# RWKV block 0's front beside the projections, its inverses inside attention, attention's norm behind scan round 0

## The reference

```python
h = rms_norm(x) * (1 + sc1) + sh1
z = h @ w_in[l]
q_lat, kv_lat, k_pe = _split(z_mla, MLA_SIZES)
z_rwkv = centred_token_shift(z_rwkv, rwkv_mu[l])
r, k, v, xw_f, xw_b, xa_f, xa_b, xg = _split(z_rwkv, RWKV_SIZES)
y_mla = mla_group(...)     # per head softmax(q k) v, then rms_norm(o, out_norm)
y_rwkv = rwkv7_group(...)  # both directions:
#   w = exp(-exp(-softplus(-(w0 + tanh(xw) @ w2)) - 0.5)); a = sigmoid(a0 + xa @ a2)
#   k_d = k * (1 + (a - 1) * k_a); kk = k * k_k / |k * k_k|
#   state = state * w + (state @ -kk) (kk * a)^T + v k_d^T;  y = state @ r
x = x + gt1 * (jnp.concatenate([y_mla, y_rwkv], axis=-1) @ w_out[l])
h = rms_norm(x) * (1 + sc2) + sh2
x = x + gt2 * conv_ffn(h, ffn_w_up[l], ffn_conv_w[l], ffn_conv_b[l], ffn_w_down[l])
```

## Time and profile before

| | us |
|---|---|
| median of three runs | 1809.8 |
| lowest, highest | 1809.66, 1811.24 |
| the profiled execution | 1816.97 |
| its span | 1815.0 |
| TensorE busy in the span | 1625.1 (90%) |
| VectorE | 1013.9 (56%) |
| ScalarE | 737.1 (41%) |
| GpSimd | 289.7 (16%) |
| its mean granted TensorE clock | 0.948 |

### The profile page before, as it was taken

One profiled execution on the slowest core, in us unless ns is written; L12 is line 12 of the kernel. 1 busy time (PEld: TensorE's weight loads), 2 busy tenths in 40 slices (PEclk: granted clock), 3 DMA queues, 4 the chain that ended last, 5 costly groups with the idle time before them and its releaser, 6 DMA issues.

```text
span 1815.0 us, 29245 instructions
## 1 busy us (share of the span) xinstructions
PE 1625.1 (90%) x11880; PEld 1189.7 (66%) x11880; DVE 1013.9 (56%) x1533; ACT 737.1 (41%) x1203; POOL 289.7 (16%) x124
## 2 busy tenths in 40 slices
PE   2899877888989999989989988598889899999997
PEld 0776434656768888877757744266667688887885
DVE  6664669886336767754334243778841544445233
ACT  3443254665543322222234343457653333323222
POOL 1333000000122222212304310000003122222121
PEclk8899987999999999999989999699999999999999
DMA  7354210000225555533303310000003222222221
GB/s 302 115 183 163 84 47 1 3 2 2 77 87 185 186 185 185 185 128 131 137 23 119 93 55 1 1 3 3 3 2 116 70 93 92 92 92 92 93 92 70
DMA packets 34659, 163.08 MB, mean 90 GB/s; under 512 B 3841, under 2 KB 4097, under 8 KB 25857
## 3 DMA queue, kind: packets, MB, share of 16 engines
q1 hardware_dynamic: 34560, 161.65, 25.5%
HBM read 159.54 MB, written 2.10 MB: 89 GB/s over the span
## 4 chain that ended last, share of the span: by engine, by line
PE 55%; issue 28%; DVE 8%; ACT 4%; POOL 4%; DMA 0%; POOLq 0%; DVEq 0%; ACTq 0%
PE bank L505 8%; PE bank L507 7%; PE bank L506 7%; PE bank_pair L505 3%; PE bank_pair L507 3%; PE bank_pair L506 3%; POOL work_parts L1932 2%; PE bank L552 2%; PE bank L852 2%; PE bank L853 2%; POOL proj_weights_parts L1927 2%; PE bank_pair L609 1%; PE bank L830 1%; PE bank L666 1%; PE bank L868 1%
## 5 line engine op out<-in xcount | busy, mean ns | idle before, releaser
L505 PE MATMUL bank<-work_parts,y_mix_parts 128*128 128x512 f32 x792 | 316.1, 399 | 20.6 <-DVE work_parts L1698 10.3
L507 PE MATMUL bank<-work_parts 128*128 128x512 f32 x792 | 315.5, 398 | 0.0
L1711 DVE TENSOR_TENSOR work_parts<-work,y_mix_parts 128x1024 fp32r<-128x1024 f32 x66 | 169.6, 2569 | 257.8 <-ACT y_mix_parts L982 257.8
L1927 POOL TENSOR_TENSOR proj_weights_parts<-proj_weights,proj_weights_hi_parts 128x1024 fp32r<-128x1024 f32 x54 | 130.4, 2422 | 884.5 <-ACT proj_weights_hi_parts L978 796.0
L1932 POOL TENSOR_TENSOR work_parts<-work,y_mix_parts 128x1024 fp32r<-128x1024 f32 x66 | 159.1, 2410 | 608.5 <-ACT y_mix_parts L982 608.5
L982 ACT ACTIVATE y_mix_parts<-work 128x1024 fp32r<-128x1024 f32 x132 | 133.0, 1054 | 263.3 <-DMA work<-mlp_dram 253.6
L506 PE MATMUL bank<-work_parts,y_mix_parts 128*128 128x512 f32 x528 | 209.0, 396 | 0.0
L505 PEld LDWEIGHTS bank<-work_parts,y_mix_parts 128*128 128x128 f32 x792 | 150.6, 190 | 58.3 <-issue 24.0
L507 PEld LDWEIGHTS bank<-work_parts 128*128 128x128 f32 x792 | 150.4, 190 | 35.9
L505 PE MATMUL bank<-work_parts,proj_weights_hi_parts 128*128 128x512 f32 x272 | 112.5, 413 | 26.6 <-DVE work_parts L1698 24.4
L506 PEld LDWEIGHTS bank<-work_parts,y_mix_parts 128*128 128x128 f32 x528 | 100.5, 190 | 24.4
(11 more groups left out here) (279 smaller groups left out, 2991.0 us busy)
## 6 DMA issues: line engine op xcount, KB each, us to landing
work<-mlp_dram SPq DMA_DIRECT2D x66, 1024.0 KB, 4.9
work<-ada_dram SPq DMA_DIRECT2D x64, 512.0 KB, 4.7
proj_weights<-tiles_dram SPq DMA_DIRECT2D x57, 512.0 KB, 3.6
x_res<-ada_dram SPq DMA_DIRECT2D x24, 512.0 KB, 4.6
x_res<-x_dram SPq DMA_DIRECT2D x2, 2048.0 KB, 10.7
mixer_inputs<-ada_dram SPq DMA_DIRECT2D x8, 512.0 KB, 17.6
work<-mlaw_dram SPq DMA_DIRECT2D x4, 640.0 KB, 5.2
out_dram<-x_res SPq DMA_DIRECT2D x8, 256.0 KB, 2.2
```

The source lines that it names most:

```text
L505: mm(out, w_hi, x_hi, start=start, stop=False)
L507: return mm(out, w_lo, x_hi, start=False, stop=stop)
L1711: TTT(MW_L[q][:, 1], MW_IN[q][:, 1], plain(MW_H[q][:, 1]), ALU.subtract).then_inc(msp_v.sem, msp_v.one("l1"))
L1927: pool.tensor_tensor(ring_l[s], ring[s], plain(ring_h[s]), ALU.subtract).then_inc(spl_q.sem, spl_q.one(f"t{s}"))
```

## The change

Four things, the same in both layers:

- **Front of block 0 beside the projections.** `rwkv_early` of block 0 runs on TensorE ahead of tiles k of b = 1 and r of b = 2, in banks 7 and 0 (`EARLY_BANK`). ScalarE's and VectorE's steps of the front follow between the tiles of b = 1 to 3. The key norm of block 0 is taken at once; logarithms and exponentials of blocks 1 to 3 come behind the last tile. The low-rank weights are loaded at tile 5.
- **Inverses of block 0 and front of block 1 inside attention.** Pair 0: both triangles, the bonus product and the inverse from `inverse_in` to `inverse_32_mid`, in pieces at the end of VectorE's steps 3 to 9. Pair 1: the rest of the inverse in steps 0, 3 and 8, the running sums of block 1 in 1 and 2, its `rwkv_early` and exponentials, and `level_turn` ahead of the last product. K and V are copied out of PSUM by ScalarE instead of VectorE. The probabilities lie in the tile buffers `RING`, so three tiles of the output projection are loaded behind attention instead of ahead, and two of them are split in the last scan round. Both products with v use bank 4, the second behind the copy of the first.
- **No round -1.** Scan round 0 starts behind `level_rest`.
- **Norm of attention behind round 0.** Its squares are taken in round 0 (chunks 2, 3, 5, 6), sums and logarithm at the round's end in place of `keep_clock`, the exponential in round 1, the scalings in round 3 and `y_head` / `y_rest` behind them.

```diff
@@ TensorE, projections
+                        if b == 1 and i == 1:
+                            pe.wait_ge(lora_in, (l + 1) * 16)
+                            pe.wait_ge(in_a.sem, in_a.at("txw", l))
+                            pe.wait_ge(sta_a.sem, sta_a.at("ln2", l))
+                            rwkv_early(first, 0, 0)
+                        if b == 2 and i == 0:
+                            rwkv_early(first, 0, 1)
@@ TensorE, attention
+                    pe.wait_ge(att_a.sem, att_a.at("v1", it))
+                    if hp == 0:
+                        rwkv_triangle(first, 0)
+                    else:
+                        rwkv_early(first + 1, 1, 0)
                     pe.wait_ge(att_v.sem, att_v.at("rp3", it))
...
+                        if hp == 0 and i == 1:
+                            rwkv_triangle(first, 1)
+                        if hp == 0 and i == 4:
+                            rwkv_bonus(first)
+                        if hp == 1 and i == 3:
+                            rwkv_early(first + 1, 1, 1)
+                        if hp == 1 and i == 9:
+                            pe.wait_ge(att_a.sem, att_a.at("pt6", it))
+                            level_turn(first)
                         if i in (6, 9):
                             e = i // 9
                             pe.wait_ge(att_a.sem, att_a.at(f"pt{4 * e + 3}", it))
+                            if e:
+                                pe.wait_ge(att_v.sem, att_v.at("o0", it))
...
-                for cur in range(-1, RB):
+                pe.wait_ge(att_v.sem, att_v.at("o1", l * 2 + 1))
+                scan_gram(first, 0)
+                scan_tokens(first, 0, 0)
+                level_rest(first, 0, True)
+                for cur in range(RB):
                     rwkv_round(l, cur, cur + 1)
@@ TensorE, end of a round
+                    pe.wait_ge(sc_a.sem, sc_a.at(f"SA{NCH - 1}", it))
+                    if cur == 0:
+                        out_norm_sums(l)
...
+                    if cur == 0:
+                        pe.wait_ge(on_a.sem, on_a.at("ln", l))
+                    else:
+                        keep_clock(new, "join", 3)
+                    level_turn(new)
+                    level_rest(new, nxt, early)
@@ VectorE, attention
+                        if l == 0 and hp == 1 and i in (4, 6):
+                            ada_rest(8 + i // 2)
+                        if hp == 0 and i < 3:
+                            kk_norm(1 + i)
                         if 1 <= i < 9:
...
+                        if hp == 0:
+                            if i == 3:
+                                inverse_in(first)
+                                inverse_half(first)
+                            if i == 4:
+                                inverse_8(first, 1, 5)
+                            if i == 5:
+                                inverse_8(first, 5, 8)
+                                inverse_16_first(first)
+                            if i == 6:
+                                bonus_end(first, 0)
+                                inverse_16_second(first)
+                            if i == 7:
+                                inverse_16_end(first)
+                            if i == 8:
+                                inverse_32_first(first)
+                            if i == 9:
+                                inverse_32_mid(first)
+                        else:
+                            if i == 0:
+                                inverse_32_second(first)
+                            if i in (1, 2):
+                                decay_sum(first + 1, i - 1)
+                            if i == 3:
+                                inverse_32_end(first)
+                            if i == 8:
+                                for p in range(2):
+                                    for e in range(2):
+                                        dve.memset(XT[p][64 * e + 32:64 * e + 64, :, :, 0:32], 0.0).then_inc(lane_v, 1)
+                                inverse_out(first)
@@ ScalarE, rounds
+                    if cur == 0 and s in (2, 3, 5, 6):
+                        out_norm_square(l, (2, 3, 5, 6).index(s))
+                    if cur == 1 and s == 6:
+                        out_norm_scale(l)
...
+                    if not build and s in (0, 2):
+                        split_tile(l, NPROJ + s // 2)
+                    if not build and s in (1, 3, 5):
+                        if s == 1:
+                            act.wait_ge(on_v.sem, on_v.at("y3", l))
```

More of the change, by code:

```diff
@@ L567, in rwkv_level, with level_rest @@
                     own(lev_p, last, f"X{d}")
+            def level_rest(it, b, early):
                 scan_gram(it, 1)
@@ L589, in rwkv_level, with out_norm_sums @@
                 scan_tokens(it, b, 1)
+            def out_norm_sums(l):
+                for i in range(4):
+                    pe.wait_ge(on_a.sem, on_a.at(f"sq{i}", l))
+                    mm(PS[1][:, :], ones, ON_SQ[i], start=(i == 0), stop=(i == 3)).then_inc(on_p.sem, on_p.one(f"s{i}"))
             pairs = [(d, e) for d in D2 for e in range(2)]
@@ L742, in rwkv_round @@
                         tail_gate(old, cur - 1)
-                if scan:
-                    own(sc_p, last, "Y")
+                own(sc_p, last, "Y")
                 if build:
@@ L1833, in _ @@
+                    if l == 0 and hp == 0:
+                        ada_rest(8)
+                        ada_rest(9)
+                scan_ring(first, 0)
+                edge(l, 0, True)
+                for cur in range(RB):
+                    rwkv_round(l, cur, cur + 1)
                 dve.wait_ge(mod_kept, 20 if l == 0 else l * 24 + 24)
```

370 lines of the change are left out of this document (203 added, 167 removed).

## The result

The changed kernel takes 1760.8 us (median of 4 runs, 1758.3 to 1763.8) and the kernel before, on the same chip, 1810.5 us (1809.7 to 1812.1): ratio 0.9725, 95% interval 0.9705 to 0.9745. It is faster by 49.8 us; 1754.3 was predicted, with 1733 to 1780 as the range. The profiled executions differ by 58.0 us (spans 1815.0 and 1757.0).

A forecast was written before the change was run, and what follows sets the result against it. Projections and nearly attention were TensorE-bound; behind attention a serial chain left it waiting. Savings of 47.5 and 50.4 us less added costs gave -23.2 and -32.3, together -55.5 us from 1809.8: 1754.3 us, range 1733 to 1780.

The forecast's parts named there:

- What was removed: Stretch from attention's last copy to scan round 0: only about 9.2 us remain, removing 47.5 us in layer 0, 50.4 in layer 1.
- The margin of the front's last VectorE part: Behind the last projection: this 6.7 us part costs nothing, with margin under 1 us, in layer 1 3 us.
- Pair 0: First head pair of attention: VectorE's pieces delay the last scaling +6.1 and +3.9 us, half clock 1.7: +7.8 and +5.6.
- Pair 1: Second head pair of attention: VectorE's pieces, the wait before `level_turn` and slow clock stretch it by +12.3 and +8.3 us.
- the new wait: End of the second head pair: TensorE waits about 5 us for the inverse's transpose before `level_turn`, last product queued behind.
- The scan rounds: Scan rounds of each layer: the moved norm and weight splits add 2.5 us a layer, between 0 and 6.
- The term for round 3: Scan round 3: two weight-tile splits replace two head copies beside step 1's table load, where ScalarE arrives last: +1.2 us.
- The term for the join: Join of scan rounds 0 and 1: norm squares, four full products replacing clock keepers, and a table load: net +1.0 us.
- (D): ScalarE's table switches on or near the path: six cost 1.4 us more than shown, +8 us, 1762; chance 0.08.
- (E): Inverse inside attention: pieces show in full, 22.4 us instead of 6 to 10 a layer, +24 us, 1778; chance 0.05.
- (C): Attention: TensorE's clock falls to 1.2 GHz in a third of the four pairs, +31 us, 1785; chance 0.12.
- (A): Attention: stretched by VectorE's pieces as laid out in the main estimate, 1754 us; chance 0.52.

The follow-up runs named there:

- second profile: The changed kernel, unedited, run and profiled again beside the kernel before: ratio 0.9732 (0.9702 to 0.9762), 1763.0 us, span 1755.3.

## Why the prediction was right, and where it was not

**The direction and the mechanism** held step by step. What was removed came out within 0.6 us in both layers (-46.9 and -50.5 against -47.5 and -50.4): only the gram, the tokens and `level_rest` stand between the copy and round 0. The margin of the front's last VectorE part held too: the path from the last projection to the first score is as long as before, 14.3 us in both kernels, so all that comes ahead of attention comes in the projections, +2.3 and +2.5 us for the 1.7 charged.

**Pair 0** (+7.8 and +5.6 predicted; +7.1 and +3.8, second profile +6.4 and +2.1) is right as a sum and wrong in its two terms. The last scaling ends 28.7 and 26.7 us after the first score in both profiles, against 24.6 before: VectorE's share is +4.1 and +2.1, and I had charged +6.1 and +3.9. With the clock kept and nothing else changed, the whole pair is 4.1 us (34.5 - 30.4) and 2.4 us longer than before, which agrees. The 2.0 us too many do not lie in the pieces. From the third score on the trace shows no idle time of VectorE up to the last scaling, and its own work, the pieces and the conditioning take 25.5 us between the first maximum and the last scaling, where I had laid out 25.7. They lie at the start: I took the 2.9 us from the first score to the first maximum and 2 us of waiting from the kernel before, whose first scores ran at a lowered clock. The changed kernel has 2.0 and 1.1. The scores and the first maximum before, then the maximum after:

```profile
180.82 1.14 PE L852 MATMUL bank<-work 128*128 128x512 f32 x2 [2.11 <-DVE work L1797]
181.78 1.88 PE L853 MATMUL bank<-work 128*128 128x512 f32 x2
183.45 1.90 PE L852 MATMUL bank<-work 128*128 128x512 f32 x2
```
```profile
183.70 0.69 DVE L1801 TENSOR_REDUCE neg_max<-bank 128x1 f32<-128x512 f32 x1 [2.94 <-PE bank L853]
```
```profile
185.15 0.69 DVE L1932 TENSOR_REDUCE neg_max<-bank 128x1 f32<-128x512 f32 x1 [2.08 <-PE bank L887]
```

The clock's share at the pair's end is 37.5 - 34.5 = 3.0 us in layer 0 and 1.4 in layer 1 (second profile: 2.2 and none), where I had 1.7 for each. The two errors have opposite signs, so that the sum came out is in part luck.

**Pair 1** (+12.3 and +8.3; +12.9 and +7.4): the new wait is what the experiments show most clearly: a wait of 4.01 us ahead of `level_turn`, then 1.86 and 6.16 us of slowed work (5.86 in layer 1) for the 1.9 and 6.7 charged. Taking the wait away brings 5.9 and 3.7 us. The last scaling ends 27.6 us after the first score in layer 0 (second profile) and 25.6 in layer 1, where I had 27.6 and 25.1. In the first profile it ends after 29.2 in layer 0, since the clock also fell in the middle of the pair: the two rows of one score, 1.02 us each elsewhere, took 1.91 and 1.36. The two conditioning pieces, charged with 2.5 us, cost 2.1: 27.6 against 25.6 with them out, and 34.0 against 31.9 us for the pair with the clock kept.

**The scan rounds** (2.5 us a layer; 1.0 and 2.7, second profile 0.3 and 5.7). The term for round 3 (1.2 us) is seen in the traces: the two head copies that the splits push aside now stand behind the table load and ahead of the copy that the scan waits for, and TensorE waits 1.71 us where it had waited 0.68. Layer 1, before and then the second profile after:

```profile
1342.38 0.38 PE L666 MATMUL bank<-rstd,work 64*64 64x64 f32 x5 [0.68 <-ACT rstd L1115]
```
```profile
1280.23 1.15 ACT L1185 ACTIVATE work_parts<-y_mix 128x512 fp32r<-128x512 f32 x2
1281.27 0.28 ACT L1160 ACTIVATE rstd<-bank 128x128 f32<-128x128 f32 x1
1281.60 0.38 PE L674 MATMUL bank<-rstd,work 64*64 64x64 f32 x5 [1.71 <-ACT rstd L1160]
```

The kernel without the norm keeps this order and has the same 1.71 us. The term for the join (1.0 us) is not seen: with the norm left out the time is the same, and the first part of the rounds moves by 2.5 us between two profiles of the changed kernel (37.4 and 34.9 in layer 0). The rounds got longer by 3.7 and 6.0 us over both layers, so the rest of it, beyond two times 1.0 us, is the clock's or not explained. In round 3 of layer 1 the second profile stands at a granted clock of 0.72 and 0.83 in places where the kernel without the norm has 0.86 and 1.00, and a part of the rounds takes 42.3 us at 1.00 and 44.0 at 0.96 in one kernel or another. The rounds also go against what attention gains: over both layers they take 354.8 us before, 358.5 and 360.8 in the changed kernel, 360.3 and 359.5 in the two experiments that leave the order in pair 1 as it is (no norm; the multiplications alone), and 361.3 to 367.0 in all the others. No run shows why.

**The rivals.** (D) is out: a table load in the changed kernel ends where the next instruction begins, as in the earlier trace rows:

```profile
170.21 1.28 ACT L1323 ACT_TABLE_LOAD   x1
171.50 0.69 ACT L1323 ACTIVATE work<-bank,constants 128x512 f32<-128x512 f32 x1
```

The further drain of 1.38 us that the Trainium skill, "ScalarE: Activation LUTs", section "What ACT_TABLE_LOAD costs", states is not seen here: 170.21 + 1.28 = 171.49, and the activation ahead of the load ends at its start as well. So it is for 39 of the 41 loads of this trace, with 0.01 or 0.02 us behind them; the other two have 1.59 and 1.07 us. (E) is out as a case of its own: with the inverse in the open the kernel is 21.9 us slower. (C) came true in the clock and not in its price. I had written that a clock below 0.9 in attention would speak for it, and it stood at 0.86 and 0.84. Those figures, with 0.95 and 0.87 in layer 1, mean that a quarter of the four pairs' time stood at the half clock, 1.2 GHz ((1 - 0.86) / 0.5 = 0.28 of pair 0, and so on), not far from the third that (C) supposed. But it cost little: 3.0 and 1.4 us in the two pairs 0, and by the slowed rows (`level_turn`, last product, in layer 0 the scores in the middle) 4.8 and 2.9 in the two pairs 1. These 12 us (an estimate) are close to the 11 that (A) had charged, and not 31 more, since most of the time at the half clock lies at the pairs' ends, where TensorE is waiting for part of it.
The Trainium skill, "TensorE: Matmul & The Clock Gate", section "What's actually happening", states that the throttled clock is the default and activity releases it; the four products at 3.70 us with four idle multiplications ahead of each agree.

**The size.** The sum of the stages, 57.7 us by the first profile, fits the spans (58.0) and is near the 55.5 predicted; the medians say 49.8 us. The difference lies in the executions that were profiled: before's took 1816.97 us, 7.2 above its median of 1809.8, and after's 1758.92, 1.8 below its own. I had subtracted a sum read from the first from the median and called the gap small beside the change; a gap of 0.4% is 7 us, about the size of the miss (1754.3 for 1760.8).

## What to carry to other kernels

Serial work of one engine can be laid beside another engine's work for little (here some 3 of 21 us a layer were left), but the order in which each piece enters the queues decides: a piece whose result another engine waits for in order (here `level_turn` ahead of the last product) belongs behind the last thing on the path, and pieces that nobody waits for belong where their engine waits anyway. When a stretch of TensorE becomes bound by another engine, read the granted clock there before and after: a few multiplications into a free bank can keep it, if no long wait stands between them and the work. And a gain in one stage is not yet a gain in time: read the later stages too.

## What the hardware showed that I had not expected

The same eight multiplications of 128x512 took 3.70 us or anything from 5.2 to 6.7, behind nearly the same waits and within one kernel: the last product of pair 0 in layer 1 took 5.38 us in one profile of the changed kernel and 3.70 in the other. With multiplications in the gaps ahead, and no wait directly before, it was 3.69 or 3.70 in all four pairs of both profiles.

The clock's pattern in the rounds can repeat exactly: in the two profiles with the clock kept in attention the four parts of layer 0's rounds took 37.9, 51.1, 44.0 and 52.5 us both times. But it need not. In layer 1 of the same two profiles they took 37.4, 48.0, 44.3, 51.8 and then 34.7, 49.4, 44.7, 52.4, and in layer 0 of the changed kernel's two profiles the first two took 37.4 and 48.0, then 34.9 and 50.2. So a stage far from an edit can move by 2 to 3 us, in one and the same kernel too, and nothing in its code says why.
